# Queries and keys handled one token tile at a time, with the last Newton steps on GpSimd and the 256-column unit projected four steps sooner

## The reference, cut to what matters

```
h = RMSNorm(x)                                   # 512 x 1024
[q, k, v | q, kv(cmp,slc,win) | gates] = h @ W_in
q, k = rms_norm over each head's 64 columns, times a gain
logits = q @ k^T / 8 + bias[head, bucket(distance)]   # own / slc / win / cmp
y = softmax(masked logits) @ v
```

## Time and profile before

| | us |
|---|---|
| median of 3 runs (lowest, highest) | 957.08 (955.17, 957.62) |
| the profiled execution | 955.18 |
| its span, first to last instruction | 953.4 |
| time around the span (955.18 - 953.4) | 1.8 |
| PE busy | 901.3 (95%) |
| DVE, ACT, POOL busy | 436.1, 408.0, 403.3 |
| attention loop, first bias to last | 101.2 to 425.1 |

### The profile page before, as it was taken

One profiled execution on the slowest core, in us unless ns is written; L12 is line 12 of the kernel. 1 busy time (PEld: TensorE's weight loads), 2 busy tenths in 40 slices (PEclk: granted clock), 3 DMA queues, 4 the chain that ended last, 5 costly groups with the idle time before them and its releaser, 6 DMA issues.

```text
span 953.4 us, 13152 instructions
## 1 busy us (share of the span) xinstructions
PE 901.3 (95%) x4585; PEld 775.5 (81%) x4585; DVE 436.1 (46%) x969; ACT 408.0 (43%) x857; POOL 403.3 (42%) x413
## 2 busy tenths in 40 slices
PE   6998898997989899999999999999999999999998
PEld 6897798896969777778778788888888888888886
DVE  5617657657475665553541654433333442021134
ACT  5222555454454555563343464444444443232231
POOL 4632323324242324365646174554444445454450
PEclk8998999997989989999999999999999999999999
DMA  5755234125012122336653073333333333332314
GB/s 167 161 144 144 50 84 114 41 79 125 20 33 57 45 56 78 125 120 242 208 168 99 22 231 94 96 99 103 106 94 97 100 89 110 92 97 89 99 56 133
DMA packets 101363, 99.31 MB, mean 104 GB/s; under 512 B 15956, under 2 KB 76084, under 8 KB 101300
## 3 DMA queue, kind: packets, MB, share of 16 engines
q1 hardware_dynamic: 101247, 98.48, 35.7%
q10 hardware_dynamic: 53, 0.01, 0.0%
HBM read 87.58 MB, written 10.88 MB: 103 GB/s over the span
## 4 chain that ended last, share of the span: by engine, by line
PE 80%; DVE 11%; ACT 4%; issue 3%; DMA 1%; POOL 0%; SPq 0%; DVEq 0%; ACTq 0%; POOLq 0%
PE banks L1488 24%; PE banks L1490 24%; PE banks L1489 24%; PE banks L1631 2%; PE banks L1542 1%; DVE plain_arena L1238 1%; PE banks L1611 1%; PE banks L1610 1%; DVE plain_arena L1118 1%; ACT split_arena L975 1%; DVE plain_arena L1266 1%; DMA plain_arena<-in_x_dram 1%; PE banks L1568 1%; PE banks L1505 1%; DVE plain_arena L1119 1%
## 5 line engine op out<-in xcount | busy, mean ns | idle before, releaser
L1488 PE MATMUL banks<-split_arena 128*128 128x512 f32 (+4 forms) x1228 | 467.0, 380 | 8.5 <-DVE split_arena L1170 4.7
L1490 PE MATMUL banks<-split_arena 128*128 128x512 f32 (+4 forms) x1228 | 456.7, 372 | 0.0
L1489 PE MATMUL banks<-split_arena 128*128 128x512 f32 (+4 forms) x1228 | 456.7, 372 | 0.0
L692 POOL TENSOR_TENSOR split_arena<-plain_arena,split_arena 128x512 fp32r<-128x512 f32 x184 | 241.1, 1322 | 255.0 <-ACT split_arena L912 235.7
L1488 PEld LDWEIGHTS banks<-split_arena 128*128 128x128 f32 x1228 | 233.2, 190 | 47.1 <-DVE split_arena L1170 5.7
L1490 PEld LDWEIGHTS banks<-split_arena 128*128 128x128 f32 x1228 | 233.2, 190 | 35.4
L1489 PEld LDWEIGHTS banks<-split_arena 128*128 128x128 f32 x1228 | 233.6, 190 | 32.2
L912 ACT ACTIVATE split_arena<-plain_arena 128x512 fp32r<-128x512 f32 x184 | 113.1, 628 | 192.7 <-PE banks L1490 184.8
L1446 DVE SCALAR_TENSOR_TENSOR plain_arena<-banks,plain_arena 128x511 f32<-128x511 f32 x44 | 32.7, 743 | 133.2 <-ACT plain_arena L1017 133.2
L871 ACT ACTIVATE plain_arena<-plain_arena 128x128 f32<-128x128 f32 (+1 forms) x96 | 53.6, 559 | 77.3 <-DVE plain_arena L1266 76.9
L707 POOL TENSOR_SCALAR plain_arena<-plain_arena 128x128 f32<-128x128 f32 (+1 forms) x64 | 38.8, 608 | 98.9 <-DVE plain_arena L1283 98.8
(11 more groups left out here) (161 smaller groups left out, 824.2 us busy)
## 6 DMA issues: line engine op xcount, KB each, us to landing
plain_arena<-in_w_up_dram SPq DMA_DIRECT2D x88, 256.0 KB, 3.1
plain_arena<-in_w_down_dram SPq DMA_DIRECT2D x44, 256.0 KB, 2.6
plain_arena<-in_w_in_dram SPq DMA_DIRECT2D x18, 512.0 KB, 4.8
plain_arena<-in_w_in_dram SPq DMA_DIRECT2D x32, 192.0 KB, 3.3
plain_arena<-in_x_dram SPq DMA_DIRECT2D x8, 512.0 KB, 5.2
gates<-plain_arena SPq DMA_DIRECT2D x16, 256.0 KB, 2.3
plain_arena<-skew SPq DMA_DIRECT2D x16, 256.0 KB, 3.9
plain_arena<-gates SPq DMA_DIRECT2D x16, 256.0 KB, 3.6
```

What stands on the lines that cost most here:

```text
L692: pool.tensor_tensor(W2l[:, c % RING, :], raw2[:, c % RING, :], W2h[:, c % RING, :].bitcast(F32), ALU.subtract).then_inc(w2_lo, 1)
L1488: nc.tensor.matmul(o, ah, bh, start=first, stop=False)
L1489: nc.tensor.matmul(o, ah, bl, start=False, stop=False)
L1490: return nc.tensor.matmul(o, al, bh, start=False, stop=last)
```

## The change

The four vectors of a unit are no longer handled one by one for all tokens. For each token tile, PE turns all four vectors (4 transposes, as many in all as before), and ACT and DVE write their high and low parts in two groups (queries, keys) or three (queries and two keys with their own gains). New tables place two first guesses a unit (ROOT), four normalisations (TILE) and four turns (TURN). The turns of a tile stand last in PE's step, and the first guess of eight numbers stays on DVE while all three Newton steps of them, twelve chained operations, run on POOL, behind everything else of its step. Unit 6 is split one step sooner and projected four steps sooner.

For units 3 to 5, with b0 the first step of pair w - 2: ROOT at b0 - 1 and b0 + 2, TILE at b0, b0 + 2, b0 + 4, b0 + 6, TURN at b0 + 1, b0 + 3, b0 + 5, b0 + 7. Unit 2: ROOT 0 and 2, TILE 1, 3, 4, 6, TURN 2, 4, 5, 7. Unit 6: SPLIT 25 to 28, PROJ 28 to 35, ROOT 32 and 36, TILE 33, 35, 38, 40, TURN 34, 36, 39, 41. Unit 7: PROJ as before, ROOT 51 and 59, TILE 52, 54, 61, 63, TURN 53, 55, 62, 64.

```diff
         elif w == 6:
-            start, counts, row = b0, (4,) * 8, 0
+            start, counts, row = b0 - 4, (4,) * 8, 0
...
-        split0 = {6: b0 - 6, 7: b0 - 8}.get(w, b0 - 7)
+        split0 = b0 - 8 if w == 7 else b0 - 7
...
-        NORM[end], VALUES[end] = w, w
-        for x in range(nvec(w)):
-            VEC[end + 2 + (w >= 6) + x] = (w, x)
+        VALUES[start + len(counts)] = w
+        ends = [t for t in sorted(PROJ) if PROJ[t][0] == w for r in range(*PROJ[t][1:]) if r % KT == KT - 1]
+        for half in range(2):
+            t = ends[2 * half + 1] + 1 if w > 2 else b0 + 2 * half
+            ROOT[t] = (w, half)
+            for a in range(2):
+                TILE[t + 1 + half + 2 * a], TURN[t + 2 + half + 2 * a] = (w, 2 * half + a), (w, 2 * half + a)
...
+            def root(w, half):                                    # POOL, last in its step
...
+                pool.wait_ge(guess_done, number + 1)
+                for i in range(3):
+                    done = 12 * number + 4 * i
+                    pool.tensor_tensor(a, y, y, ALU.mult).then_inc(root_done, 1)
+                    pool.wait_ge(root_done, done + 1)
+                    pool.tensor_tensor(a, a, v, ALU.mult).then_inc(root_done, 1)
+                    pool.wait_ge(root_done, done + 2)
+                    pool.tensor_scalar(a, a, -0.5, 1.5, ALU.mult, ALU.add).then_inc(root_done, 1)
+                    pool.wait_ge(root_done, done + 3)
+                    pool.tensor_tensor(y, y, a, ALU.mult).then_inc(root_done, 1)
+                    if i < 2:
+                        pool.wait_ge(root_done, done + 4)
...
-                if w > 1 and tt == 0:
-                    act.wait_ge(norm_done, 2 * (w - 1))
+                if w > 1:
+                    act.wait_ge(norm_done, 2 if w == 2 else norm_number(w - 1, tt))
...
+            def tile_high(w, tt):                                 # ACT, ahead of exp(t)
...
+                for v0, v1, kind, sl, g in vec_groups(w):
+                    dst = QQ[sl][:, :, q] if kind == "q" else Kh[:, sl, v0 - 2:v1 - 2, q]
+                    ins = nc.scalar.activation(dst, PS[:, 1, P * v0:P * v1].rearrange("p (v c) -> p v c", v=v1 - v0), ACT.Copy, scale=cst[:, g:g + 1])
...
+            def guess(w, half):                                   # DVE
+                c = slice(8 * half, 8 * half + 8)
+                dve.wait_ge(ss_done, NT * (w - 2) + 2 * half + 2)
+                if w > 2:
+                    dve.wait_ge(norm_done, norm_number(w - 1, 2 * half + 1))
+                first_guess(rq[:, c], st[:, 40:56][:, c], st[:, 60:76][:, c], ss[:, c], 1.0 / DH, guess_done)
+            def normalise(w, tt):                                 # DVE
+                dve.wait_ge(root_done, 12 * (2 * (w - 2) + tt // 2 + 1))
...
+                nc.vector.tensor_tensor(o, i, r, ALU.mult).then_inc(norm_done, 1)
...
# DVE, one step of the loop (bias and invert as before)
+                for done in proj_end(t):
+                    sums(*done)
                 if t >= LAG:
                     pt_low(t - LAG)
-                if t - 1 in NORM:
-                    rstd_end()
-                    normalise(NORM[t - 1], 0)
-                    normalise(NORM[t - 1], 1)
+                if t - 1 in TURN:
+                    tile_low(*TURN[t - 1])
+                if t in SPLIT:
+                    w_low(*SPLIT[t])
+                if t in TILE:
+                    normalise(*TILE[t])
+                if t in ROOT:
+                    guess(*ROOT[t])
...
+            def turn_tile(w, tt):                                 # PE, last in its step
+                pe.wait_ge(vec_lo, vec_number(w, tt) - 5)
+                pe.wait_ge(norm_done, norm_number(w, tt))
+                for v in range(4):
+                    ins = nc.tensor.transpose(PS[:, 1, P * v:P * (v + 1)], qn[:, tt, v, :], ident)
```

More of the change, by code:

```diff
@@ L1123, in newton, with rsqrt @@
                     link(ins)
-            def rsqrt_begin(y, src, inv_n, wdt, parts=P):
+            def rsqrt(y, src, inv_n, wdt, parts=P):
                 v, a = st[0:parts, 40:40 + wdt], st[0:parts, 60:60 + wdt]
[L1128 to L1142, removed]
+                first_guess(y, v, a, src, inv_n)
+                for _ in range(3):
+                    newton(y, v, a)
             def w_high(w, kts):
@@ L1224, in rstd_end, with norm_first @@
[L1224 to L1233 removed]
+            def norm_first():
+                dve.wait_ge(sq_done, 1)
+                link(nc.vector.reduce_sum(ss.rearrange("p (t v) -> p t v", t=NT), sq.rearrange("p t (v c) -> p t v c", v=4), AX))
+                rsqrt(rq[:, 0:16], ss, 1.0 / DH, 16)
+                dve.wait_ge(cmp_hidden, 2)
@@ new lines, in norm_first @@
+                for half in range(2):
+                    v = slice(half, 4, 2)
+                    for a in range(2):
+                        ins = nc.vector.tensor_tensor(qn[:, :, v, a * DH:(a + 1) * DH], i[:, :, v, :],
+                                                      r[:, :, v].unsqueeze(3).broadcast_to([P, NT, 2, DH]), ALU.mult)
+                    ins.then_inc(norm_done, 1)
+            def guess(w, half):
+                c = slice(8 * half, 8 * half + 8)
+                dve.wait_ge(ss_done, NT * (w - 2) + 2 * half + 2)
+                if w > 2:
+                    dve.wait_ge(norm_done, norm_number(w - 1, 2 * half + 1))
+                first_guess(rq[:, c], st[:, 40:56][:, c], st[:, 60:76][:, c], ss[:, c], 1.0 / DH, guess_done)
@@ new lines, in tile_low @@
+            def tile_low(w, tt):
+                q = slice(P * tt, P * (tt + 1))
+                dve.wait_ge(vec_hi, vec_number(w, tt) - 4)
+                for v0, v1, kind, sl, g in vec_groups(w):
+                    r0 = DH if kind == "q" else 0
+                    hi = QQ[sl][r0:P, :, q] if kind == "q" else Kh[:, sl, v0 - 2:v1 - 2, q]
+                    dst = hi if kind == "q" else Kl[:, sl, v0 - 2:v1 - 2, q]
+                    ins = nc.vector.scalar_tensor_tensor(out=dst, in0=PS[r0:P, 1, P * v0:P * v1].rearrange("p (v c) -> p v c", v=v1 - v0),
+                                                         scalar=cst[r0:P, g:g + 1], in1=hi.bitcast(F32), op0=ALU.mult, op1=ALU.subtract)
+                ins.then_inc(vec_lo, 1)
@@ L1720, in _ @@
                     gate(*GATE[t])
+                if t in TURN:
+                    turn_tile(*TURN[t])
             def turn_x(tt):
```

165 lines of the change are left out of this document (65 added, 100 removed).

## The result

| | before | after |
|---|---|---|
| median of 4 runs, us | 956.12 (954.88 to 957.62) | 942.15 (940.69 to 943.29) |
| ratio, 95% interval | | 0.985 (0.9835 to 0.9866) |
| profiled execution, us | 955.18 | 943.29 |
| its span, us | 953.4 | 941.3 |

The kernel is 14.0 us faster by the medians. The forecast was 952, a gain of 4 to 5 us; the time lies inside the range of 936 to 966, and the sign was right. The two profiled executions differ by 11.9 only: the one of before is among the fastest of its runs, the one of after is the slowest of its four.

A forecast was written before the change was run, and what follows sets the result against it. PE bounds the kernel through idle time and low clock. Pairs sum -1.5 + 0 + 0 + 6.7 + 0 = 5.2 us won, 955.2 to 950.0 profiled; with 1.9 for the median, 952, range 936 to 966.

The forecast's parts named there:

- What bounds the kernel: PE, busy 901.3 of 953.4 us; only its idle time and clock can win, some 36 us at most.
- The chain: Twelve linked Newton operations on POOL, twice a unit: 4.1 us plus 0.3 for meetings with DVE, 4.4 us.
- The clock: PE at 1.2 GHz behind holes, one time in two: 3.4 us stretches, 1.7 lost each, 20 to 25 us in all.
- Pairs 3 and 4: Together 11.8 us won, 5.8 from unit 6's moved rows; three low-clock stretches take 5.1 off, leaving 6.7 won.
- The step-34 hole: In pair 4, a tile's turn waits for guess 3.0, chain 4.4 and product 0.8: hole 2.4 us.
- Pair 0: First chain has nothing hiding it; later bias(6) and half a chance of another low clock: 1.5 us lost.
- pairs 1 and 2: A 2.5 us hole on POOL replaces 2.7 on DVE; tile turned earlier against possible low clock: 0 net.
- Pair 5: Hole of 5.1 us before the scaling, against DVE's peak gone: taken as 0, between 3 lost and 3 won.
- About 7 us on each us of chain: Rate over the loop: two chains count in pair 0, one in each of pairs 1 to 5.
- The rival that the chain hides: POOL's Newton chain lasts 3.0 us instead of 4.4, 10 won plus 4 of clock: 938 us, chance 0.27.
- Slower: Rival: DVE shuts POOL out during the twelve operations, chain 6.2 us: 965 us, decides from 5.1 a chain; chance 0.22.
- Nothing moves: Rival: DVE sets the pace of pair 4's steps 36 to 43, 6.7 won falls to 2: 957 us, chance 0.16.

The follow-up runs named there:

- pad4: Changed kernel with each Newton chain on POOL lengthened from 12 to 16 operations by repeating its first product: 959.45 us.
- vlow_later: Changed kernel with POOL's subtraction for the values' low part (v_low) issued three steps later: 938.85 us.
- pad2: Changed kernel with each Newton chain on POOL lengthened from 12 to 14 operations: 953.95 us.
- gate_behind: Changed kernel with POOL's gate-weight split placed behind its projection-weight split in the same step: 940.42 us.
- both: Changed kernel with the values' subtraction three steps later for units 2, 3, 4 and 7, and the gate split behind the projection-weight split: 933.03 us.

## Why the prediction was right and wrong

- **What bounds the kernel: right.** The gain is holes (6.5 us) and low clock (8.3 us). POOL had 31.1 us more to do, and the kernel became faster.
- **The chain, "12 x (0.20 + 0.14)" and 0.3 for meetings, 4.4 us: wrong, 3.3 to 3.9 measured.** The 0.20 was right. The wait is 0.08 and not 0.14: it was read from additions of 512 columns (L782), and the link between operations of 8 columns is shorter. A meeting with DVE costs 0.3, in four chains of twelve. This is the step that failed, as a term that was mis-sized: every place named for a hole was right but step 39, and the holes were 1.7 where 2.5 stood. With 4 more operations, 1.1 us, the same kernel is 17.3 us slower (pad4).
- **The clock, "one time in two" behind a hole of 2.5, three low stretches in pairs 3 and 4: the number of stretches wrong, the chance not.** With the short chain the clock fell in no pair but the last: 6.8 us of low clock where 20 to 25 were forecast. Over the fourteen profiles, 1.2 GHz came with 8 of 13 holes of 2.0 to 2.6 us, near the half that was taken, but with only 4 of 18 holes of 1.64 to 1.79, and the holes were of that length. A stretch of 3.4 us cost 1.5 and not 1.7.
- **What a chain of 4.4 us costs: too small, hidden by the short chain.** pad4, with the chain that was assumed, is 7.5 us above the 952: pairs 0 to 2 lose 8.5 where the sum has 1.5 lost, and pair 5 1.7 where it has 0. The forecast is as near as it is because this error and the one of the chain have opposite signs.
- **Pairs 3 and 4, 11.8 won before the clock, less 5.1: the first near, the second not.** They won 12.5, and no stretch of theirs was at 1.2 GHz. The step-34 hole of 2.4 was 0.55, the one of step 39 is not there, and step 29 has one hole of 1.65 for the two of 1.9 and 2.6. This is 5.8 of the 9.5 us by which the loop beat its sum.
- **Pair 0, 1.5 lost: 0.4 won; pairs 1 and 2, 0: 1.0 and 1.2 won.** Another 4.1 of the 9.5, with no stretch of these pairs at 1.2 GHz.
- **Pair 5, 0 between 3 lost and 3 won: right,** 0.4 lost. Its hole was 4.66 for 5.1, and vlow_later shows what it was worth: 5.1 us.
- **About 7 us on each us of chain: wrong as a rate.** The measured slopes are 5, 21 and about 10. The rival that the chain hides, 938, came nearest, 4 us away: the measured chain lies about midway between its 3.0 us and the 4.4, and its gain of clock is what happened, though the chain is not hidden.
- **Slower, from 5.1 us a chain: possible, its point too far out.** The kernel is as slow as before already between an undisturbed chain of 3.9 and one of 4.5 us (pad2 and pad4). The meetings with DVE that it feared for the twelve operations took place behind them, on the scaling (1.52 for 0.70).
- **Nothing moves (pair 4 at DVE's pace): fell.** Pair 4 has the length of its PE work and 2.5 us of holes.

Open is why the clock falls behind some holes of one length and not behind others: two kernels with the same hole of 2.03 us in step 30 differ in it (gate_behind and both), and no run sets this apart from everything else. Open is also how much of a hole's effect stands in the medians, since each kernel was profiled once.

## What to carry to other kernels

Price a wait by an operation of the same size: the link between tiny operations is not the one between wide ones, and a dozen of them in a row turn 0.06 us into most of a microsecond. A hole of PE has a second price in the clock, and here it rose steeply with the length, from 4 holes in 18 at 1.7 us to all at 2.7: when several copies of the same hole stand in that range, a small error in its length moves them all, so forecast the time for both lengths. Before an engine is given more work at the end of its step, look at what stands ahead of it there that nobody wants yet; moving that away gained 9.1 us here, two thirds as much as the change.

## What the runs showed of the hardware

A linked operation on 128x8 numbers costs GpSimd 0.20 us and 0.08 us of wait, whether with one tensor input (L723) or two (L719, L721, L725):

```profile
L725 POOL TENSOR_TENSOR plain_arena<-plain_arena 128x8 f32<-128x8 f32 x36 | 8.1, 226 | 3.0
L721 POOL TENSOR_TENSOR plain_arena<-plain_arena 128x8 f32<-128x8 f32 x36 | 7.7, 214 | 2.8
...
L723 POOL TENSOR_SCALAR plain_arena<-plain_arena 128x8 f32<-128x8 f32 x36 | 7.1, 198 | 3.3
```

On DVE an integer operation of the first guess took 1.21 us for eight numbers beside POOL's value split and ended with it (147.45 to 148.66, the split to 148.64), and the next one 0.17: for tiny work the meeting cost more than the operation.

The granted clock can be held against PE's single holes in the loop, over all fourteen profiles of this case. A hole is counted as one with low clock when a stretch at 1.2 GHz begins in it or at most 1.6 us behind it:

| holes of | number | with 1.2 GHz |
|---|---|---|
| 1.25 to 1.48 us | 45 | 0 |
| 1.64 to 1.79 us | 18 | 4 |
| 2.01 to 2.59 us | 13 | 8 |
| 2.71 us and more | 33 | 33 |

This is a count of what came together, not a rule with a threshold: in after, one stretch at 1.2 GHz (from 332.56) stands behind no hole longer than 0.75.
